# The first modulation of a two-layer diffusion step: pairs of modulation tiles go through TensorE amid the first chunk of the input projection

## The chip, the cores and the metric

The kernel runs on one core of a Trainium2 chip. Its engines work side by side, each through its own list of instructions, and wait for each other on semaphores: TensorE (PE) multiplies matrices into PSUM, VectorE (DVE) and ScalarE (ACT) work element by element, GpSimd (POOL) helps, and SyncE (SP) issues most of the transfers (DMA). The metric is the device time of one execution in microseconds, lower is better; the time of a kernel is the median of several runs.

## The reference

One step of a backbone with two layers over 512 latent and 128 context tokens (640 in all) of width 1024. What matters here is how a layer begins:

```python
def adaln(cond, w_ada, b_ada):
    m = jax.nn.silu(cond) @ w_ada + b_ada
    return jnp.split(m[:, None, :], 6, axis=-1)
def modulate(x, g, shift, scale):
    return rms_norm(x, g) * (1 + scale) + shift
...
        sh_a, sc_a, g_a, sh_f, sc_f, g_f = adaln(c, w_ada[l], b_ada[l])
        h = modulate(xs, norm_mix_g[l], sh_a, sc_a)
        q_mla, c_kv, k_rope, na_q, na_k, na_v, gq, gk, gv = mixer_inputs(
            h, w_in[l], mla_q_norm_g[l], mla_kv_norm_g[l], w_q_up[l], gqa_q_norm_g[l], gqa_k_norm_g[l])
```

There are two conditions, `c` for the latent tokens and `c_ctx` for the context tokens. `m` has 6 x 1024 features, here 48 tiles of 128: tiles 0 to 7 are the shift and tiles 8 to 15 the scale of the first norm. The input projection `h @ w_in` takes 1024 features to 1824 columns.

## The kernel before

All activations are kept with features on the partitions: `x` is eight feature tiles of 128 x 640. `h` goes into `hT` as two parts, a high one and a low one (`h` minus the high part), and so do the weights (`wi`), and every dense product is three matmuls (`split_mm`, lines 773 to 775: high x high, high x low, low x high). The projection has six chunks of 304 columns. Chunk 0 runs feature tile by feature tile over five row tiles of 128 tokens, in five banks of PSUM, so tile k can be used as soon as `h_ready` says that it is there; it has 8 x 5 x 3 = 120 matmuls. Chunks 1 to 5 run row tile by row tile, 24 matmuls each.

A modulation tile is 128 features of `m` for both conditions. There are two ways to get it. VectorE's `ada(l, t)` (L1672) multiplies the tile's weights, 128 x 1024, with the silu of one condition, which lies on every partition (`silu_c`), and adds up along the row: two dots for a tile. TensorE's way is a product with the condition as the weights of two columns (`silu_k`) and 256 features streaming past it over eight feature tiles of the input: a row of 256 results on two partitions (`ada_rows`, L914). ScalarE copies the row from PSUM (L1405), and a small product with the identity turns it into columns (`rows_to_columns`, L922). In float32 each such product is two passes, so eight products stand as 16 in the trace.

In the opening of layer 0 ten of the 16 tiles (`BY_PE = 10`) go through TensorE as five pairs and six (`FIRST`) through VectorE. ScalarE squares `x`, VectorE adds the squares up (L1825, L1828), TensorE sums over features (`token_sums`, L781), ScalarE takes the root, VectorE the reciprocal, and TensorE spreads it over all partitions (`spread_rstd`, L789). Then VectorE adds the bias to all 16 tiles at once, makes the scale (`coefs`), and `modulated` makes tn = x times the reciprocal (L1719), hf = tn * coef + shift (ScalarE L1294, or VectorE L1726 for tiles 0, 4 and 7), the high part (L1302) and the low part (L1657). Loads of the opening stand in SP's queue by hand: pairs, `x`, the six tiles' weights and the first chunk's weights in turn.

During chunks 1 to 5 VectorE computes 24 more modulation tiles (`REST`), a group for each chunk (`REST_AT`), behind the split of that chunk's weights (`wi_split`).

Of the kernel before, what the change touches and what calls it, by code (L numbers as in the profile page):

```python
# [25 lines left out]
P = 128  # L26
# [25 lines left out]
RING1, RING2 = 8, 3  # L52
BY_PE = 10
FIRST = list(range(BY_PE, ADA1))
GATE = list(range(40, NADA))
REST = list(range(ADA1, GATE[0]))
REST_AT = [0, 0, 5, 10, 15, 20, 24]
# [3 lines left out]
ORDER = [list(range(BY_PE, NADA)), NEXT + REST]  # L61
# [11 lines left out]
NORM_BANK = [5, 3, 1, 3, 1]  # L73
# [163 lines left out]
def build(nc, a, out):  # L237
    ctx = ExitStack()
    with ctx:
# [57 lines left out]
        s7 = ExitStack()  # L297
        ada_n = sb("ada_n", [P, BY_PE // 2, KD, 2 * P], F32, s7)
        s7.close()
# [32 lines left out]
        ada_w1 = sb("ada_w1", [P, RING1 - RING2, DM], F32, s2)  # L332
        sb("pad_z", [P, NT * IN_COLS - 6 * T - (RING1 - RING2) * DM], F32, s2)
# [15 lines left out]

        s4 = ExitStack()  # L350
# [15 lines left out]
        spare = ada_w1[:, len(FIRST) - RING2:, :].rearrange("p a b -> p (a b)")  # L366
        silu_k = spare[:, BY_PE * P:BY_PE * P + 2 * KD].rearrange("p (k q) -> p k q", q=2)
        rows = spare[0:2, 0:BY_PE * P]

# [11 lines left out]
        ada_n_in = [sem(f"ada_n_in{i}") for i in range(BY_PE // 2)]  # L381
        rows_ps = sem("rows_ps")
        rows_done = sem("rows_done")
        acc_first = sem("acc_first")
        ada_n_ps = sem("ada_n_ps")
        silu_done = sem("silu_done")
        ada_in = [sem(f"ada_in{i}") for i in range(RING1)]
# [133 lines left out]
        def ring_of(l, t):  # L521

            if l and t not in REST:
                return 2, NEXT.index(t)
            return (RING2, t - ADA1) if t in REST else (RING1, t - BY_PE)

        def ada_slot(l, t):

            slot = slot_of(l, t)
            if l == 0 and t >= GATE[0] and slot >= 6:  # L530
                where = ada_g[:, slot - 6]
            elif slot < 2:
                where = ada_w[:, slot]
            elif slot < RING2:
                where = ada_wq[:, slot - 2]
            else:
                where = ada_w1[:, slot - RING2]
            return where, ada_in[slot], 16 * (len(slot_users(l, t)) + 1), dot_at(l, t)

        def slot_of(l, t):  # L540

            if l == 0 and t >= GATE[0]:
                return (6, 7, 0, 1)[(t - GATE[0]) % 4]
            ring, n = ring_of(l, t)
            return n % ring

# [70 lines left out]
        def _(sp):  # L617
# [30 lines left out]
            for l in range(DEPTH):  # L648

                if l == 0:  # L650
                    def ada_n_load(i):
                        sp.dma_start(ada_n[:, i], a["w_ada_first"][i]).then_inc(ada_n_in[i], 16)

                    def x_load(i):
                        sp.dma_start(x[:, 4 * i:4 * i + 4, :], a["x"][4 * i * P:4 * (i + 1) * P, :]
                                     .rearrange("(k p) n -> p k n", p=P)).then_inc(x_in[i], 16)
                    sp.dma_start(silu_k, a["condT"]).then_inc(cond_k_in, 16)
                    ada_n_load(0)
                    sp.dma_start(silu_c[:], a["cond"].unsqueeze(0).broadcast_to([P, 2, DM])).then_inc(cond_in, 16)
                    ada_load(0, FIRST[0])  # L660
                    ada_load(0, FIRST[1])
                    x_load(0)
                    ada_n_load(1)
                    ada_load(0, FIRST[2])
                    x_load(1)
                    ada_load(0, FIRST[3])
                    ada_n_load(2)
                    ada_load(0, FIRST[4])
                    ada_n_load(3)
                    wi_load(l, 0)  # L670
                    ada_n_load(4)
                    ada_load(0, FIRST[5])
# [7 lines left out]
                if l:  # L680
# [4 lines left out]
                    sp.wait_ge(cond_in, 48)  # L685
# [9 lines left out]
                for c in range(1, IC):  # L695
# [4 lines left out]
                    for t in REST[REST_AT[c]:REST_AT[c + 1]]:  # L700
                        ada_load(l, t)
# [69 lines left out]
        def _(pe):  # L771
# [136 lines left out]
            def ada_rows(pair):  # L908

                pe.wait_ge(ada_n_in[pair], 16)  # L910
                if pair >= 2:
                    pe.wait_ge(rows_done, pair - 1)
                for k in range(KD):
                    m = pe.matmul(ps[0:2, 2 + 2 * (pair % 2), 0:256], silu_k[:, k], ada_n[:, pair, k, :],  # L914
                                  start=k == 0, stop=k == KD - 1, skip_group_check=True)
                m.then_inc(rows_ps, 1)

            def rows_to_columns(pair):

                pe.wait_ge(rows_done, pair + 1)  # L920
                for t in range(2 * pair, 2 * pair + 2):
                    m = pe.matmul(ps[:, 3, 2 * t:2 * t + 2], rows[:, t * P:(t + 1) * P], ident[0:2, 0:2],  # L922
                                  start=True, stop=True, skip_group_check=True)
                m.then_inc(ada_n_ps, 1)

            pe.wait_ge(ones_set, 1)
            for l in range(DEPTH):
                if l == 0:
                    pe.wait_ge(silu_k_done, 1)
                    for pair in range(3):  # L930
                        ada_rows(pair)
                    pe.wait_ge(acc_first, KD - 1)
                    token_sums(0, rstd, True, True).then_inc(ss_done, 1)
                    ada_rows(3)
                    pe.wait_ge(const_in, 16 * 5)
                    for pair in range(3):
                        rows_to_columns(pair)
                    spread_rstd(0)
                    ada_rows(4)
                    for pair in range(3, 5):  # L940
                        rows_to_columns(pair)

                for c in range(IC):
                    pe.wait_ge(wi_ready, l * IC + c + 1)
                    if c == 0:

                        for k in range(KD):
                            pe.wait_ge(h_ready, l * 2 * KD + k + 1)
                            for t in range(NT):
                                m = split_mm(ps[:, t, 0:ICW], hT[:, k, 0, t * P:(t + 1) * P], hT[:, k, 1, t * P:(t + 1) * P],  # L950
                                             wi[:, 0, 0, k, :], wi[:, 0, 1, k, :], k == 0, k == KD - 1)
                                if k == KD - 1:
                                    m.then_inc(z_ps, 1)
                        continue
# [303 lines left out]
        def _(sc):  # L1258
# [23 lines left out]

            def modulated(l, nrm):
                base = l * 2 * KD + nrm * KD
                own = (2 * l + nrm) * (KD - len(HF_DVE))
                sc.wait_ge(coef_done, l * 2 + nrm + 1)
                for k in range(KD):
                    sc.wait_ge(tn_ready, base + k + 1)
# [9 lines left out]
                    else:  # L1298
# [3 lines left out]
                        sc.activation(hT[:, k, 0], own_hf, ACT.Copy).then_inc(h_hi, 1)  # L1302

# [87 lines left out]
            for l in range(DEPTH):  # L1391
                if l == 0:
                    sc.wait_ge(cond_k_in, 16)
                    sc.activation(silu_k, silu_k, ACT.Silu).then_inc(silu_k_done, 1)
                    for dst, src in ((b_ada, a["b_ada"]), (norm_g, a["norm_g"]), (ident, a["ident"]), (fin_g, a["fin_g"]),
                                     (qn_g, a["qn_g"])):
                        sc.dma_start(dst[:], src).then_inc(const_in, 16)
                    sc.wait_ge(cond_in, 16)
                    sc.activation(silu_c[:], silu_c[:], ACT.Silu).then_inc(silu_done, 1)
# [3 lines left out]
                    def rows_out(pair):  # L1403
                        sc.wait_ge(rows_ps, pair + 1)
                        sc.activation(rows[:, 256 * pair:256 * pair + 256], ps[0:2, 2 + 2 * (pair % 2), 0:256], ACT.Copy).then_inc(rows_done, 1)  # L1405

                    def first_square(k):
                        if k >= 2:
                            sc.wait_ge(acc_first, max(1, k - 2))
                        sc.activation(sq[:, k % 2], x[:, k], ACT.Square).then_inc(sq_ready, 1)  # L1410
# [974 lines left out]
```

## Time and profile before

| | |
|---|---|
| median of 3 runs | 1703.88 us (1703.1 to 1705.22) |
| the profiled execution's own time | 1701.98 us |
| its span, first to last instruction | 1700.2 us |
| mean granted TensorE clock | 0.985 |
| TensorE busy | 1631.1 us (96%) |
| VectorE busy | 1310.9 us (77%) |
| ScalarE busy | 781.5 us (46%) |
| moved by DMA | 223.79 MB, mean 132 GB/s |

The busy shares are means over stages that differ. What a change of the opening is worth is read from the order of events in the opening, and from whether the stages behind it wait for TensorE, VectorE or a transfer. A time in a row is counted from the start of the span.

### The profile page before, as it was taken

What the parts mean: (1) busy time and instruction counts of PE and PEld (TensorE: products, weight loads), DVE (VectorE), ACT (ScalarE), POOL (GpSimd) and SP (SyncE); (2) the same over time, 40 slices, a digit from 0 to 9 for tenths busy, and PEclk for the clock granted to TensorE, in tenths of its full rate; (3) what the DMA queues carried; (4) which work ended last, traced back from release to release, by engine and by line L of the source; (5) the groups of instructions that cost most, each with busy time, mean ns of one, the idle gap of its engine ahead of it and who ended that gap; (6) DMA issues with size and microseconds to landing.
All of it is one profiled execution on the core that took longest, in us unless ns stands there. A gap on an engine that the chain in (4) does not pass through costs nothing.

```text
span 1700.2 us, 28338 instructions
## 1 busy us (share of the span) xinstructions
PE 1631.1 (96%) x10942; PEld 1560.1 (92%) x10942; DVE 1310.9 (77%) x2309; ACT 781.5 (46%) x1489; POOL 398.5 (23%) x438
## 2 busy tenths in 40 slices
PE   6999989999999999999999989999999999999997
PEld 2998878889999999999999977888999999999997
DVE  5897788877988888888869877887387777677764
ACT  3534767852633333333352476687363333333332
POOL 0033554310012221212114073632001221121111
PEclk8999999999999999999989999999999999999998
DMA  9562000065177777777537310001606666666651
GB/s 369 193 229 65 10 3 1 1 218 167 40 181 193 207 202 191 188 192 195 161 131 241 118 45 1 3 1 39 198 1 156 178 148 162 153 175 166 154 129 62
DMA packets 114138, 223.79 MB, mean 132 GB/s; under 512 B 7488, under 2 KB 39040, under 8 KB 113024
## 3 DMA queue, kind: packets, MB, share of 16 engines
q1 hardware_dynamic: 90800, 177.90, 30.5%
q0 software_dynamic: 22240, 44.14, 15.6%
q8 instruction: 49, 0.80, 0.2%
q10 hardware_dynamic: 1008, 0.61, 0.1%
q14 instruction: 41, 0.34, 0.1%
HBM read 218.01 MB, written 3.57 MB: 130 GB/s over the span
## 4 chain that ended last, share of the span: by engine, by line
PE 84%; DVE 8%; ACT 3%; issue 2%; DMA 1%; POOL 1%; SPq 1%; POOLq 0%; DVEq 0%; ACTq 0%
PE ps L773 24%; PE ps L775 24%; PE ps L774 24%; DVE ps L1672 3%; PE ps L1041 3%; PE ps L1011 1%; PE ps L781 1%; PE ps L1013 1%; PE ps L858 1%; PE ps L816 1%; DMA ada_n<-in_w_ada_first 1%; DVE hT L1657 1%; DVE negmax L1909 1%; PE ps L914 1%; PE ps L796 1%
## 5 line engine op out<-in xcount | busy, mean ns | idle before, releaser
L773 PE MATMUL ps<-act,dhi 128*128 128x320 f32 x704 | 217.8, 309 | 0.0
L775 PE MATMUL ps<-act,dlo 128*128 128x320 f32 x704 | 217.5, 309 | 0.0
L774 PE MATMUL ps<-act,dhi 128*128 128x320 f32 x704 | 217.5, 309 | 0.0
L2036 DVE SCALAR_TENSOR_TENSOR x<-ps,mod,x 128x512 f32<-128x512 f32 x352 | 170.4, 542 | 42.4 <-PE ps L775 42.4
L773 PE MATMUL ps<-hS,whi 128*128 128x320 f32 x640 | 197.8, 309 | 0.0
L774 PE MATMUL ps<-hS,whi 128*128 128x320 f32 x640 | 197.8, 309 | 0.0
L775 PE MATMUL ps<-hS,wlo 128*128 128x320 f32 x640 | 197.8, 309 | 0.0
L1657 DVE TENSOR_TENSOR wlo<-wraw,whi 128x1024 fp32r<-128x1024 f32 (+3 forms) x166 | 192.0, 1166 | 5.1 <-POOL wraw L2296 5.1
L773 PE MATMUL ps<-hT,whi 128*128 128x320 f32 x608 | 188.0, 309 | 2.2 <-DVE hT L1657 2.2
L775 PE MATMUL ps<-hT,wlo 128*128 128x320 f32 x608 | 187.9, 309 | 0.0
L774 PE MATMUL ps<-hT,whi 128*128 128x320 f32 x608 | 187.9, 309 | 0.0
L1562 ACT ACTIVATE whi<-wraw 128x1024 fp32r<-128x1024 f32 (+1 forms) x160 | 146.8, 946 | 50.2 <-POOL wraw L2296 18.6
L773 PE MATMUL ps<-wi,hT 128*128 128x304 f32 x480 | 146.6, 305 | 4.7 <-DVE hT L1657 4.1
L775 PE MATMUL ps<-wi,hT 128*128 128x304 f32 x480 | 146.0, 304 | 0.0
L774 PE MATMUL ps<-wi,hT 128*128 128x304 f32 x480 | 145.5, 303 | 0.0
L588 POOL TENSOR_SCALAR probs<-probs,rinv 128x640 f32<-128x640 f32 (+2 forms) x128 | 101.8, 796 | 149.5 <-DVE rinv L569 148.4
L773 PEld LDWEIGHTS ps<-act,dhi 128*128 128x128 f32 x704 | 132.1, 188 | 0.6 <-DVE x L2036 0.5
L774 PEld LDWEIGHTS ps<-act,dhi 128*128 128x128 f32 x704 | 132.2, 188 | 0.0
L775 PEld LDWEIGHTS ps<-act,dlo 128*128 128x128 f32 x704 | 132.2, 188 | 0.0
L2296 POOL TENSOR_TENSOR wraw<-wraw 128x512 f32<-128x512 f32 x40 | 63.7, 1592 | 271.3 <-PE ps L775 109.4
L1657 DVE TENSOR_TENSOR pT<-ps,pT 128x512 fp32r<-128x512 f32 (+2 forms) x176 | 109.1, 621 | 14.7 <-ACT pT L1494 13.8
L774 PEld LDWEIGHTS ps<-hS,whi 128*128 128x128 f32 x640 | 120.1, 188 | 0.0
(265 smaller groups left out, 4331.3 us busy)
## 6 DMA issues: line engine op xcount, KB each, us to landing
ada_w<-in_w_adaT SPq DMA_DIRECT2D x65, 512.0 KB, 5.1
draw<-in_w_down SPq DMA_DIRECT2D x22, 1024.0 KB, 6.0
wraw<-in_up_q SPq DMA_DIRECT2D x22, 768.0 KB, 6.6
wraw<-in_gate_q SPq DMA_DIRECT2D x20, 768.0 KB, 4.4
wraw<-in_gate_q POOLq DMA_DIRECT2D x20, 768.0 KB, 7.2
wraw<-in_up_q POOLq DMA_DIRECT2D x20, 768.0 KB, 7.1
wi_raw<-in_w_in SPq DMA_DIRECT2D x12, 1216.0 KB, 6.9
wraw<-in_gate_q SPq DMA_DIRECT2D x20, 512.0 KB, 3.4
```

The lines of the kernel that those rows point to most:

```text
L588: po.tensor_scalar(t, t, rinv[:, u:u + 1], 1.0, ALU.mult, ALU.mult).then_inc(p_ready, 1)
L773: pe.matmul(dst, lh, rh, start=start, stop=False, skip_group_check=True)
L774: pe.matmul(dst, lh, rl, start=False, stop=False, skip_group_check=True)
L775: return pe.matmul(dst, ll, rh, start=False, stop=stop, skip_group_check=True)
L781: m = pe.matmul(ps[:, bank, 2 * t:2 * t + 2], tile[:, t * P:(t + 1) * P], ones[:, 0:2], start=first and t == 0, stop=last, skip_group_chec ...
L796: pe.matmul(ps[:, bank, 0:tile.shape[-1]], tile[:, 0:P], tile, start=True, stop=True, skip_group_check=True)
L1041: m = pe.transpose(ps[:, 4 + n % 2, i * P:(i + 1) * P], probs[:, g % 2, i, pos:pos + P], ident[:])
L1562: sc.activation(whi[:, g], wraw[:, g], ACT.Copy).then_inc(quarter_hi[m], 1)
L1657: return ve.tensor_tensor(dst, src, f(hi), ALU.subtract)
L1672: i = ve.scalar_tensor_tensor(out=junk, in0=w, scalar=1.0, in1=c[:, q], op0=ALU.mult, op1=ALU.mult, accum_out=mod[:, l, t, q:q + 1])
L2036: i = ve.scalar_tensor_tensor(out=x[:, o, c0:c1], in0=y[:, 512 - HALF + c0:512 - HALF + c1], scalar=mod[:, l, 5 * KD + o, q:q + 1], in1=x[ ...
L2296: po.tensor_tensor(wraw[:, 7 * m + S4], wraw[:, 7 * m + S2], wraw[:, 7 * m + A12], ALU.add).then_inc(s4_done[m], 1)
```

## The change

- All 16 tiles of the first norm go through TensorE, as eight pairs of another make: pair k has shift tile k and scale tile 8 + k, the two that feature tile k of `h` needs. The weights are stored accordingly on the host side.
- Pairs use four buffers (`SLOTS`) in turn, two in `ada_n0` and two in `ada_n1`. The load of pair k waits until the rows of pair k - 4 are done.
- Three pairs are computed ahead of chunk 0. Within it, TensorE computes the rows of pair k + 3 after feature tile k, and turns the rows of pair k + 2 between its row tiles 1 and 2. ScalarE's row copy stands behind the high part of tile k, VectorE's bias and scale of tile k + 1 ahead of the low part of tile k (`first_mod`, `first_modulated`).
- The silu of the conditions on all partitions (`silu_c`) is no longer loaded: TensorE spreads it from `silu_k` with the identity, 16 products (`spread_silu`), and ScalarE copies it out of PSUM. Keep-warm products on the identity (24, 6 and 3) are added.
- The spread reciprocal is copied from PSUM to `rstd` and read from there. The first weights are split in two halves.
- SP's queue begins with the condition, the identity and `x`, then pair 0, the first weights, and the other seven pairs.
- `REST_AT` of layer 0 moves one tile from the first group to the last.

The core of the diff:

```diff
-REST_AT = [0, 0, 5, 10, 15, 20, 24]
+REST_AT = [[0, 0, 4, 9, 14, 19, 24], [0, 0, 5, 10, 15, 20, 24]]
...
+                    sp.dma_start(silu_k[:], a["condT"]).then_inc(cond_k_in, 16)
+                    sp.dma_start(ident[:], a["ident"]).then_inc(ident_in, 16)
+                    for i in range(2):
                         sp.dma_start(x[:, 4 * i:4 * i + 4, :], a["x"][4 * i * P:4 * (i + 1) * P, :]
                                      .rearrange("(k p) n -> p k n", p=P)).then_inc(x_in[i], 16)
...
+                    first_load(0)
                     wi_load(l, 0)
-                    ada_n_load(4)
-                    ada_load(0, FIRST[5])
+                    for k in range(1, KD):
+                        first_load(k)
...
+            def first_rows(k):
+
+                pe.wait_ge(ada_n_in[k % SLOTS], 16 * (k // SLOTS + 1))
+                if k:
+                    pe.wait_ge(rows_done, k)
+                for j in range(KD):
+                    m = pe.matmul(ps[0:2, 5, 0:2 * P], silu_k[:, j], first_w(k)[:, j, :], start=j == 0, stop=j == KD - 1,
+                                  skip_group_check=True)
                 m.then_inc(rows_ps, 1)
...
+            def first_chunk(l, k):
+
+                pe.wait_ge(h_ready, l * 2 * KD + k + 1)
+                for t in range(NT):
+                    if t == 2 and l == 0 and k + 2 < KD:
+                        first_columns(k + 2)
+                    m = split_mm(ps[:, t, 0:ICW], hT[:, k, 0, t * P:(t + 1) * P], hT[:, k, 1, t * P:(t + 1) * P],
+                                 wi[:, 0, 0, k, :], wi[:, 0, 1, k, :], k == 0, k == KD - 1)
...
-                    pe.wait_ge(silu_k_done, 1)
-                    for pair in range(3):
-                        ada_rows(pair)
+                    spread_silu()
+                    keep_warm(4, ident[:], 24)
+                    first_rows(0)
                     pe.wait_ge(acc_first, KD - 1)
                     token_sums(0, rstd, True, True).then_inc(ss_done, 1)
-                    ada_rows(3)
-                    pe.wait_ge(const_in, 16 * 5)
-                    for pair in range(3):
-                        rows_to_columns(pair)
+                    first_columns(0)
+                    keep_warm(2, ident[:], 6)
                     spread_rstd(0)
-                    ada_rows(4)
-                    for pair in range(3, 5):
-                        rows_to_columns(pair)
-
-                for c in range(IC):
+                    first_rows(1)
+                    keep_warm(2, ident[:], 3)
+                    first_columns(1)
+                    first_rows(2)
+                    pe.wait_ge(wi_half_ready, 1)
+                    pe.wait_ge(mod_done, 2)
+                    for k in range(KD):
+                        if k == KD // 2:
+                            pe.wait_ge(wi_ready, 1)
+                        first_chunk(l, k)
+                        if k + 3 < KD:
+                            first_rows(k + 3)
...
+                    if l == 0 and nrm == 0 and k + 2 < KD:
+                        rows_out(k + 2)
```

TensorE's list from its first instruction to the first matmul of chunk 0, before (-) and now (+). L914 before is a product of a row, L922 a turning; now L914 is the spreading of the silu, L796 a keep-warm product, L924 a product of a row and L938 a turning:

```order
-L914 MATMUL ps<-ada_n,ada_w 2x256 x24
+L914 MATMUL ps<-ident,silu_k 128x128 x16
+L796 MATMUL ps<-ident 128x128 x24
+L924 MATMUL ps<-ada_n,silu_k 2x256 x8
 L781 MATMUL ps<-ones,rstd 128x2 x5
-L914 MATMUL ps<-ada_n,ada_w 2x256 x8
-L922 MATMUL ps<-ident,ada_w 128x2 x6
+L938 MATMUL ps<-ident,rows 128x2 x2
+L796 MATMUL ps<-ident 128x128 x6
 L789 MATMUL ps<-ident,rstd 128x128 x5
-L914 MATMUL ps<-ada_n,ada_w 2x256 x8
-L922 MATMUL ps<-ident,ada_w 128x2 x4
```

Three of the five pairs stood ahead of the sums (L781) and two behind; now one pair stands ahead of the sums. Two more of the eight follow before the chunk, and five are inside it, where before there were only the 120 matmuls.

ScalarE's list of the change from the root of the sums to the high part of tile 2 (L1316 copies a row out of PSUM, L1453 and L1455 make the high part of half the first weights, L1457 copies the spread reciprocal, L1332 and L1340 make `h`):

```order
L1309 ACTIVATE rms<-ps,eps 128x5
L1455 ACTIVATE wi<-wi_raw 128x1216
L1457 ACTIVATE rstd<-ps 128x640
L1316 ACTIVATE rows<-ps 2x256
L1460 DMA rope<-in_rope 128x768
L1460 DMA mask<-in_mask 128x160
L1332 ACTIVATE hT<-tn,mod,coef 128x512
L1332 ACTIVATE hT<-tn,mod,coef 128x128
L1316 ACTIVATE rows<-ps 2x256
L1332 ACTIVATE hf<-tn,mod,coef 128x512
L1332 ACTIVATE hf<-tn,mod,coef 128x128
L1340 ACTIVATE hT<-hf 128x640
```

Before, all row copies came ahead of the first high part; now ScalarE waits for a row after each of the tiles 0 to 5.

VectorE's list of the change from the last bias and scale to the first dots of chunk 1 (L1772 adds the bias, L1775 makes the scale, L1810 is tn, L1816 hf, L1691 the low parts):

```order
L1772 TENSOR_TENSOR mod<-ps,b_ada 128x2x2
L1775 SCALAR_TENSOR_TENSOR coef<-mod,norm_g 128x2
L1810 TENSOR_TENSOR tn<-x,rstd 128x640
L1816 TENSOR_SCALAR hf<-tn,coef,mod 128x512
L1816 TENSOR_SCALAR hf<-tn,coef,mod 128x128
L1691 TENSOR_TENSOR hT<-hf,hT 128x640 x2
L1691 TENSOR_TENSOR wi<-wi_raw,wi 128x2432
L1706 SCALAR_TENSOR_TENSOR ps,mod<-ada_w,silu_c 128x1024 x4
```

The low parts of tiles 6 and 7 (x2) come behind the bias and scale of tile 7, so behind the turning of the last pair's rows.

## Rows read from the trace of the kernel before

**Rows 1.** The page: span, and the chain that ended last by engine.

```profile
span 1700.2 us, 28338 instructions
...
PE 84%; DVE 8%; ACT 3%; issue 2%; DMA 1%; POOL 1%; SPq 1%; POOLq 0%; DVEq 0%; ACTq 0%
```

**Rows 2.** Busy time by stretch: length, PE, PEld, DVE, ACT, POOL, clock, DMA share, GB/s.

```profile
5.00:10.00 5.00, 3.68 (x9) 1.15 (x10) 0.00 (x0) 1.12 (x1) 0.00 (x0) 1.00 1.01 405
...
0.00:47.30 47.30, 29.76 (x121) 12.67 (x121) 27.16 (x42) 16.95 (x24) 0.44 (x6) 0.88 0.99 361
47.30:53.40 6.10, 6.10 (x25) 6.10 (x26) 5.20 (x9) 5.79 (x10) 0.00 (x0) 0.52 1.05 395
...
53.40:150.20 96.80, 96.80 (x697) 96.67 (x696) 88.49 (x130) 37.44 (x72) 19.51 (x18) 1.00 0.48 159
```

**Rows 3.** Timeline of TensorE in the opening: start, duration, operation, idle before.

```profile
6.32 6.52 PE L914 MATMUL ps<-ada_n,ada_w 128*2 128x256 f32 x16 [6.32 <-DMA ada_n<-in_w_ada_first]
...
26.11 5.17 PE L914 MATMUL ps<-ada_n,ada_w 128*2 128x256 f32 x16 [2.43 <-DMA ada_n<-in_w_ada_first]
...
31.21 1.28 PE L781 MATMUL ps<-ones,rstd 128*128 128x2 f32 x10
...
35.97 1.50 PE L922 MATMUL ps<-ident,ada_w 2*128 2x2 f32 x12
37.39 1.38 PE L789 MATMUL ps<-ident,rstd 128*128 128x128 f32 x10
...
47.26 0.59 PE L773 MATMUL ps<-wi,hT 128*128 128x304 f32 x1 [3.88 <-DVE hT L1657]
```

**Rows 4.** The chain that ended last: start, share in the chain, operation.

```profile
32.49 3.54 PE ps L914 x16
...
38.77 3.54 PE ps L914 x16
```

**Rows 5.** Timeline of TensorE in layer 1, at a granted clock of 0.50.

```profile
868.63 2.33 PE L789 MATMUL ps<-ident,rstd 128*128 128x128 f32 x10
```

**Rows 6.** Timeline of VectorE and ScalarE in the opening.

```profile
2.50 0.22 ACT L1394 ACTIVATE ada_w<-ada_w 128x16 f32<-128x16 f32 x1 [0.47 <-DMA ada_w<-in_condT]
...
27.24 3.61 DVE L1828 TENSOR_TENSOR rstd<-rstd,sq 128x640 f32<-128x640 f32 x4
...
31.32 0.37 ACT L1405 ACTIVATE ada_w<-ps 2x256 f32<-2x256 f32 x1 [1.56 <-PE ps L914]
...
43.78 0.17 DVE L1686 SCALAR_TENSOR_TENSOR coef<-mod,norm_g 128x16 f32<-128x16 f32 x1
...
44.90 1.20 ACT L1294 ACTIVATE hT<-tn,mod,coef 128x512 fp32r<-128x512 f32 x2 [2.18 <-DVE tn L1719]
...
46.30 0.82 DVE L1657 TENSOR_TENSOR hT<-hf,hT 128x640 fp32r<-128x640 f32 x1
...
47.64 0.74 ACT L1302 ACTIVATE hT<-hf 128x640 fp32r<-128x640 f32 x1
...
57.76 0.80 DVE L1726 TENSOR_SCALAR hf<-tn,coef,mod 128x512 f32<-128x512 f32 x2
```

**Rows 7.** Groups by line, whole span: a copy of 512 columns from PSUM.

```profile
L1336 ACT ACTIVATE K<-ps 64x512 fp32r<-64x512 f32 x36 | 21.3, 591 | 22.3 <-PE ps L775 12.5 <-PE ps L858 9.6
```

**Rows 8.** Timeline of ScalarE and VectorE, from chunk 0 to the stage's end.

```profile
58.99 2.22 ACT L1276 ACTIVATE wi<-wi_raw 128x2432 fp32r<-128x2432 f32 x1
...
61.24 2.69 DVE L1657 TENSOR_TENSOR wi<-wi_raw,wi 128x2432 fp32r<-128x2432 f32 x1 [1.22 <-ACT wi L1276]
...
70.20 0.42 ACT L1443 ACTIVATE z<-ps 128x304 f32<-128x304 f32 x1 [0.71 <-PE ps L775]
...
149.03 0.34 DVE L1884 SCALAR_TENSOR_TENSOR z<-z,stat,kv_g 128x128 f32<-128x128 f32 x1
...
150.36 0.42 ACT L1443 ACTIVATE z<-ps 128x304 f32<-128x304 f32 x1 [2.92 <-PE ps L775]
...
151.16 0.28 DVE L1657 TENSOR_TENSOR K<-kc_na,K 64x128 fp32r<-64x128 f32 x1 [1.78 <-ACT K L1310]
```

More of the change, by code:

```diff
@@ L380, in build @@
         silu_k_done = sem("silu_k_done")
-        ada_n_in = [sem(f"ada_n_in{i}") for i in range(BY_PE // 2)]
+        ident_in = sem("ident_in")
+        silu_ps = sem("silu_ps")
+        ada_n_in = [sem(f"ada_n_in{i}") for i in range(SLOTS)]
         rows_ps = sem("rows_ps")
         rows_done = sem("rows_done")
+        mod_done = sem("mod_done")
+        coef_k = sem("coef_k")
+        rstd_copied = sem("rstd_copied")
+        wi_half_hi = sem("wi_half_hi")
+        wi_half_ready = sem("wi_half_ready")
         acc_first = sem("acc_first")
@@ L386, in build @@
         silu_done = sem("silu_done")
-        ada_in = [sem(f"ada_in{i}") for i in range(RING1)]
+        ada_in = [sem(f"ada_in{i}") for i in range(5)]
         ada_done = sem("ada_done")
@@ L524, in ring_of @@
                 return 2, NEXT.index(t)
-            return (RING2, t - ADA1) if t in REST else (RING1, t - BY_PE)
+            return RING2, t - ADA1
         def ada_slot(l, t):
             slot = slot_of(l, t)
-            if l == 0 and t >= GATE[0] and slot >= 6:
-                where = ada_g[:, slot - 6]
-            elif slot < 2:
+            if slot < 2:
                 where = ada_w[:, slot]
@@ L536, in ada_slot @@
             else:
-                where = ada_w1[:, slot - RING2]
+                where = ada_g[:, slot - RING2]
             return where, ada_in[slot], 16 * (len(slot_users(l, t)) + 1), dot_at(l, t)
@@ L906, in queries, with spread_silu @@
                 m.then_inc(qm_ps, 1)
[L908 to L915, printed above, removed]
-                m.then_inc(rows_ps, 1)
[L918 to L922, printed above, removed]
+            def spread_silu():
+                pe.wait_ge(silu_k_done, 1)
+                pe.wait_ge(ident_in, 16)
+                for q in range(2):
+                    for k in range(KD):
+                        m = pe.matmul(ps[:, 2 * q + k // 4, (k % 4) * P:(k % 4 + 1) * P], silu_k[:, k, q:q + 1].broadcast_to([P, P]),
+                                      ident[:], start=True, stop=True, skip_group_check=True)
+                    m.then_inc(silu_ps, 1)
@@ new lines, in first_rows, with first_columns @@
+            def first_rows(k):
[5 more added lines that the diff above has]
+                                  skip_group_check=True)
+                m.then_inc(rows_ps, 1)
+            def first_columns(k):
+                pe.wait_ge(rows_done, k + 1)
+                if k == 0:
+                    pe.wait_ge(silu_done, 1)
+                else:
+                    pe.wait_ge(mod_done, k)
+                if k == 2:
+                    pe.wait_ge(rstd_copied, 1)
+                for half in range(2):
+                    m = pe.matmul(ps[:, FIRST_BANK[k], 2 * half:2 * half + 2], rows[0:2, k % 2, half * P:(half + 1) * P], ident[0:2, 0:2],
@@ L1281, in rms, with rows_out @@
                 sc.activation(rms5[:], sums, ACT.Sqrt, scale=1.0 / DM, bias=eps[:]).then_inc(rms_ready, 1)
+            def rows_out(k):
+                sc.wait_ge(rows_ps, k + 1)
+                if k >= 2:
+                    sc.wait_ge(ada_n_ps, k - 1)
+                sc.activation(rows[0:2, k % 2], ps[0:2, 5, 0:2 * P], ACT.Copy).then_inc(rows_done, 1)
             def modulated(l, nrm):
```

204 lines of the change are left out of this document (114 added, 90 removed).

## The prediction

> **What bounds the kernel now.** I read the profile in five steps. The chain that ended last [rows 1] lies on TensorE for 84% of a span of 1700.2 us, so a microsecond that TensorE starts its dense work later is a microsecond at the end unless something else gives way. The busy times by stretch [rows 2] show where it is not dense: in the first 47.3 us it is busy 29.8 us, from 53.4 to 150.2 us it is busy all 96.8 us, in 697 matmuls of 0.139 us each. The timeline of TensorE [rows 3] shows what the first 47 us are: five products of the condition with a pair of modulation tiles (L914, 16 passes each), three of them behind a wait for their DMA, then the sums, the spreading of the rms, the turned rows (L922), and at 47.26 us the first chunk of the input projection. ScalarE starts to copy the first row tile of chunk 1 at 70.20 us [rows 8]; that is 24 matmuls of 0.139 us or 3.34 us after chunk 1 began, so chunk 0 ended at 66.9 us. It took 19.6 us for 120 matmuls, since its first 6.1 us ran at a granted clock of 0.52 [rows 2]. From there to 150.3 us TensorE never waits. The figure to forecast is therefore the end of chunk 0, 66.9 us now.
>
> **What the change moves.** Before, five pairs (ten tiles) go through TensorE and six tiles through VectorE. Now all 16 tiles go through TensorE, as eight pairs. Three pairs stand before the chunk and five inside it. One pair takes 3.54 us at full clock [rows 4]. VectorE's twelve dots cost TensorE nothing before; the three pairs more cost it 10.6 us. Against this TensorE's waits for DMA in the opening go, the first chunk starts earlier, and it runs at full clock.
>
> **The start of the chunk.** The first wait is for the identity tile, now second on SP's queue. The condition, issued at 0.75 us, is used at 2.50 us [rows 6]; the identity is issued some 0.4 us later. I take 4.0 us, between 3.5 and 5.5. TensorE then has 16 spreads and 24 keep-warm products, 80 passes of 128 columns. At half clock such a pass takes 0.21 us (ten in 2.33 us, with 0.42 us for the last) [rows 5], at full clock 0.114 us (1.38 us for ten) [rows 3]. How long it stays at the lower level of 1.2 GHz: after a wait the row products began slow at 6.32 us and 26.11 us and the first chunk at 47.26 us [rows 3]; the group at 26.11 took 5.17 us instead of 3.54, so some 3.3 us were slow, and the chunk was slow for 6.1 us. I take 4.8 us: 22 slow passes, then 58 in 6.6 us, done at 15.4 us. The first pair follows and ends at 18.9 us. DMA is not in the way: at 405 GB/s [rows 2] x, the first pair and the first weights (4.9 MB) are in by some 16 us, the pairs follow each 2.6 us, so the third is in by 22 us.
>
> ScalarE and VectorE run beside it. Half of the spread silu is there at 7.4 us, all by 9.8 us; four copies from PSUM of 0.59 us [rows 7] end at 11.1 us. Then come eight squares and seven sums at 0.90 us each (3.61 us for four) [rows 6]: the last sum ends at 19.0 us. So both chains meet at 19 us. From there everything is in one line on TensorE: sums 1.28, two columns 0.5 (12 passes of turning take 1.50 us), twelve keep-warm passes 1.4, spreading the rms 1.3, pair two 3.54, six passes 0.7, columns 0.5, pair three 3.54. The chunk starts at 31.8 us, 15.4 us earlier than now. The rms copy on ScalarE, the first product with x, half the weight split and the first h tile end before that: by the rows of 0.74 to 0.82 us [rows 6] h of tile 0 is ready near 30.4 us.
>
> **The length of the chunk.** 120 matmuls at 0.139 us are 16.7 us, five pairs at 3.54 us are 17.7 us, six turnings at 0.5 us are 3.0 us. For tiles 0 to 4 TensorE needs 6.1 us a tile, while ScalarE needs 1.94 us for h (1.20 and 0.74) and 0.37 us for the row copy, VectorE 1.6 to 2.4 us and two small operations of 0.2 us [rows 6]; they are covered. The cover ends at tile 6. The last pair ends at 62.5 us, its row copy is followed on ScalarE by h of tile 6, and on VectorE by columns at 63.9, coefficients 0.4, tn 0.8, hf 0.8 and the low half 0.8 us: 66.7 us, where TensorE has been free since 65.1 us. That is a wait of 1.6 us. Sum 39.0 us, end of chunk 0 at 70.8 us. Weights of chunk 1 are split on ScalarE only after the last h, 2.22 us, and on VectorE, 2.69 us [rows 8]: 66.4 + 2.2 + 2.7 = 71.3 us, so TensorE waits another 0.5 us. It begins chunk 1 at 71.3 us instead of 66.9: **4.4 us later**. Moved loads: SP's queue waits for the fourth pair before the last pair's load (about 41 us), and behind it stand the weights of chunk 1, nine small tables, wq and the next tiles' loads. The weights are wanted at 66 us and the tiles at 71 us, so this costs nothing unless they come 20 us late.
>
> **After it.** VectorE begins its split at 68.6 us instead of 61.2 us, 7.4 us later, while TensorE is 4.4 us later. VectorE's 24 tiles of this stage are the same, one of them moved from the first group to the last. It ended the normalisation at 149.4 us and did its first key piece at 151.2 us [rows 8], so it had 1.8 us; it is now 3.0 us later relative to TensorE and 1.2 us late for a small piece, with more idle time right behind. I take nothing for it, with 1.2 us as the upper bound. The rest of the program waits for the end of the stage as before.
>
> Sum +4.4 us, and 0.5 us for some ten handovers between engines that I have taken as free. The profiled execution took 1701.98 us, 1.78 us over its span, and lies 1.9 us under the median of the runs, 1703.88 us. Its own time with the change would be 1706.9 us, the median 1708.8 us.
>
> **A place where rule and trace differ.** The recorded clock says 1.00 for 5 to 10 us [rows 2], yet the 16 passes that began at 6.32 us took 6.52 us [rows 3], 0.41 us each, where 16 at 2.4 GHz take 3.54 us, so the record is no help in the opening and the level was 1.2 GHz. The Trainium skill (TensorE: Matmul & The Clock Gate, What's actually happening) says that the default state is throttled and activity releases it; by that rule the opening starts slow, and the trace's pace agrees. By the rule the sum is +4.4 us, by the recorded clock the opening would be 2.2 us shorter and the sum +2.2 us.
>
> **The rivals.**
> *The clock falls once more* (chance 0.20). Near 19 us TensorE has sums and columns of two elements' width, 1.8 us, and a short wait. Before, a wait of 2.43 us at 26.11 us was enough to make the next 3.3 us slow [rows 3]; but the sums at 31.21 us, with pairs on both sides, kept full clock. If it falls, 3.4 to 5 us run at half pace: +1.7 to 2.5 us, time 1711.
> *VectorE ends the stage* (0.14). The 1.2 us above bite, or a load for its dots is late: 1710.
> *A shorter opening* (0.20). The slow stretch is short, or the wait before tile 6 vanishes because VectorE is quicker there: 1.5 to 2.5 us less, 1706 to 1707, which is no difference that can be told.
> *Faster* (0.06). The row products cost less inside the dense stream than alone, because their weights have two columns. The five would have to take 2.66 us each to break even and under 2.0 us to be faster by over 0.2%; then the time is under 1700.5. For it speaks only that none stood between dense matmuls; against it, that the two at full clock took 3.54 us each in different company [rows 4].
> *The chunk starves* because pairs arrive late: part of the slower side. The third pair has 6 us in hand at 28 us.
>
> **How the numbers follow.** The forecast itself has 0.40, with 1707 to 1710 as its own range. About 0.2% (3.4 us) is what a measurement can tell from no change. Faster 0.06; within 0.2% the shorter opening and the lowest edge of the forecast, 0.23; slower 0.71. The range goes from 1704.5 (all lower bounds: identity at 3.5, short slow stretch, no wait at tile 6) to 1713 (clock falls, identity at 5.5 us).
>
> **What would show it.** First chunk starting near 32 us; row products inside it at 3.5 us each; the chunk some 39 us long; chunk 1 starting at 71 us; a wait of one to two microseconds on the low half of h before tile 6; 4 to 5 us more in the span, all of it before 72 us. It is wrong if row products overlap with the dense matmuls, if the chunk starts before 27 us, or if the later stages give the time back.

## The result, and the profile after

The changed kernel takes 1712.64 us (median; one run of 4135 us was disturbed and is left out), the kernel before, on the same chip, 1703.1 us. The ratio is 1.0062, 95% interval 1.0049 to 1.0075, so 8.3 to 12.8 us more. The prediction said 1708.8 us. The sign was right and the time lies in the range, but the loss was forecast at 4.9 us: the medians differ by 9.5 us, about twice that.

The page of the changed kernel: span, busy time, and the chain that ended last by engine.

```profile
span 1710.2 us, 28667 instructions
...
PE 1652.5 (97%) x11100; PEld 1577.1 (92%) x11100; DVE 1294.5 (76%) x2299; ACT 784.8 (46%) x1497; POOL 395.5 (23%) x438
...
PE 84%; DVE 9%; ACT 4%; issue 2%; POOL 1%; DMA 0%; POOLq 0%; DVEq 0%; SPq 0%; ACTq 0%
```

The span grew by 10.0 us against [rows 1], and the chain still lies on TensorE. Its busy time by stretch (columns as in [rows 2]), cut at the start of chunk 0, its end, and the end of the stage:

```profile
0.00:33.40 33.40, 29.33 (x175) 22.02 (x175) 12.12 (x19) 15.84 (x24) 0.44 (x6) 0.95 0.86 318
33.40:75.00 41.60, 40.27 (x225) 26.39 (x224) 16.02 (x31) 17.45 (x30) 0.00 (x0) 1.00 0.58 192
75.00:159.00 84.00, 83.77 (x600) 83.52 (x600) 78.34 (x116) 28.73 (x61) 19.36 (x18) 1.00 0.54 178
```

Chunk 0 begins at 33.4 us instead of 47.3 and ends at 75.0 us instead of 66.7: 13.9 us are won ahead of it and some 22 lost inside it. From there to the end of the stage the distance stays the same. These are the rows of ScalarE and VectorE that answer to [rows 8]:

```profile
72.43 2.69 DVE L1691 TENSOR_TENSOR wi<-wi_raw,wi 128x2432 fp32r<-128x2432 f32 x1 [0.88 <-ACT wi L1304]
...
73.35 2.07 ACT L1477 ACTIVATE z<-ps 128x304 f32<-128x304 f32 x5 [1.02 <-PE ps L775]
...
78.83 0.42 ACT L1477 ACTIVATE z<-ps 128x304 f32<-128x304 f32 x1 [1.27 <-PE ps L775]
...
158.99 0.42 ACT L1477 ACTIVATE z<-ps 128x304 f32<-128x304 f32 x1 [2.92 <-PE ps L775]
...
160.32 0.33 DVE L1962 SCALAR_TENSOR_TENSOR z<-z,stat,kv_g 128x128 f32<-128x128 f32 x1
160.58 0.28 DVE L1691 TENSOR_TENSOR K<-kc_na,K 64x128 fp32r<-64x128 f32 x1
```

The first copy of z of chunk 1 starts at 78.83 us instead of 70.20, the last of the stage at 158.99 instead of 150.36: 8.63 us both times. So 8.6 of the 10.0 us by which the span grew arise before the first copy of chunk 1, and this copy is the marker by which the experiments below are read.

The chain that ended last shows the line on TensorE up to chunk 0 (start, share in the chain, operation):

```profile
17.97 0.84 DVE rstd L1798
18.80 0.04 issue
18.85 1.28 PE ps L781 x10
20.13 0.53 PE ps L938 x4
20.66 2.21 PE ps L796 x12
22.87 2.07 PE ps L789 x10
24.94 3.54 PE ps L924 x16
28.48 0.87 PE ps L796 x6
29.35 0.53 PE ps L938 x4
29.88 3.54 PE ps L924 x16
33.43 0.34 PE ps L773
```

The twelve keep-warm passes and the spreading of the rms took 4.28 us where 2.7 were forecast. The busy times there say why; the granted clock is the third number from the end, 0.58:

```profile
21.00:23.00 2.00, 2.00 (x13) 2.00 (x12) 0.22 (x2) 0.53 (x1) 0.00 (x0) 0.58 1.03 426
```

Inside the chunk, TensorE's timeline over one tile and the start of the next (start, duration, operation):

```profile
34.16 0.30 PE L775 MATMUL ps<-wi,hT 128*128 128x304 f32 x1
34.38 0.60 PE L938 MATMUL ps<-ident,rows 2*128 2x2 f32 x4
34.91 0.41 PE L773 MATMUL ps<-wi,hT 128*128 128x304 f32 x1
35.16 0.30 PE L774 MATMUL ps<-wi,hT 128*128 128x304 f32 x1
...
36.12 0.30 PE L775 MATMUL ps<-wi,hT 128*128 128x304 f32 x1
36.35 3.62 PE L924 MATMUL ps<-ada_n,silu_k 128*2 128x256 f32 x16
39.90 0.41 PE L773 MATMUL ps<-wi,hT 128*128 128x304 f32 x1
40.14 0.30 PE L774 MATMUL ps<-wi,hT 128*128 128x304 f32 x1
...
40.93 0.60 PE L938 MATMUL ps<-ident,rows 2*128 2x2 f32 x4
```

Read the starts, since the durations overlap. Dense matmuls start 0.14 us apart. From the last of them to the turning it is 0.22 us, and behind the turning the first takes 0.25 us until the next; the same at the row product, 0.23 and 0.24. Each change from the dense products to the narrow ones or back (a border, below) thus costs about 0.1 us, four of them 0.4 us a tile. The period of a tile is 6.55 us (34.38 to 40.93), where the forecast had 6.1.

TensorE's waits up to 170 us (in all, times, longest):

```profile
PE ps L914 <- DMA ident<-in_ident: 3.4, 1, 3.4
PE ps L773 <- DVE hT L1691: 1.3, 1, 1.3
PE ps L858 <- DVE K L1691: 0.8, 1, 0.8
PE ps L781 <- DVE rstd L1798: 0.7, 1, 0.7
...
PE ps L773 <- DVE wi L1691: 0.2, 1, 0.2
```

The 1.3 us on the low part of h are the wait before tile 6 (at 70.53 us), forecast at 1.6. No transfer is waited for inside the chunk.

### The profile page after: what moved, and what is told of

It is laid out like the page before. It is cut to its first block, busy times and chain, and to the rows that moved or that the text cites. A ratio compares the mean times of both kernels' runs of the same rounds, so it can differ in the third digit from the quotient of the medians.

```text
span 1710.2 us, 28667 instructions
## 1 busy us (share of the span) xinstructions
PE 1652.5 (97%) x11100; PEld 1577.1 (92%) x11100; DVE 1294.5 (76%) x2299; ACT 784.8 (46%) x1497; POOL 395.5 (23%) x438
## 4 chain that ended last, share of the span: by engine, by line
PE 84%; DVE 9%; ACT 4%; issue 2%; POOL 1%; DMA 0%; POOLq 0%; DVEq 0%; SPq 0%; ACTq 0%
PE ps L773 24%; PE ps L775 24%; PE ps L774 24%; DVE ps L1706 3%; PE ps L1069 3%; PE ps L924 1%; PE ps L781 1%; PE ps L1039 1%; PE ps L1041 1%; PE ps L858 1%; PE ps L816 1%; DVE negmax L1987 1%; DVE hT L1691 1%; PE ps L796 1%; ACT probs L1428 1%
## 5 line engine op out<-in xcount | busy, mean ns | idle before, releaser
L1691 DVE TENSOR_TENSOR wlo<-wraw,whi 128x1024 fp32r<-128x1024 f32 (+3 forms) x166 | 189.7, 1153 | 7.4 <-POOL wraw L2374 7.4
L1596 ACT ACTIVATE whi<-wraw 128x1024 fp32r<-128x1024 f32 (+1 forms) x160 | 148.2, 947 | 74.4 <-DMA wraw<-in_gate_q 33.4
L1691 DVE TENSOR_TENSOR pT<-ps,pT 128x512 fp32r<-128x512 f32 (+2 forms) x176 | 109.1, 621 | 14.9 <-ACT pT L1528 13.6
```

Of the source, the lines that this page charges most:

```text
L1596: sc.activation(whi[:, g], wraw[:, g], ACT.Copy).then_inc(quarter_hi[m], 1)
L1691: return ve.tensor_tensor(dst, src, f(hi), ALU.subtract)
```

## The experiments

The theory was that TensorE's own list is the cost: five pairs of 3.55 us stand in the chunk, and the rest of the miss is the clock near 20 us and the changes between products. The rivals were that the order or a wait of another engine makes the loss, and that it lies behind the first stage. "Copy" below is the start of the first copy of z of chunk 1; all ratios are to the kernel before on the same chip, with their 95% intervals. The copy comes from one execution of each version, so a difference of some tenths of a microsecond in the opening can be that execution's own.

**Four more keep-warm products.** They fill TensorE's wait for the last sum.

```
 first_rows(0)
+keep_warm(4, ident[:], 4)
 pe.wait_ge(acc_first, KD - 1)
```

> Edit: four more keep-warm products on the identity ahead of TensorE's wait for the sum of squares (18.1 to 18.85 us in the trace of the change). The trace of the change shows the keep-warm products and the spreading of the rms from 20.6 to 24.9 us at half pace, 2.28 us each instead of 1.4 and 1.3 us. Theory A (TensorE's own list is the path, and its clock fell after the wait and the narrow products): the clock stays up, the chunk starts 1.5 to 1.8 us earlier, time 1710.5 to 1711 beside 1712.6 of the change. Rival (the clock fell because of the narrow products, 1.9 us of sums and turnings, which the edit leaves): it falls all the same and the time is 1712.6 or 0.2 more.

Ratio 1.0045 (1.003 to 1.006), copy at 78.83 us, as in the change. TensorE's timeline near 21 us shows the fall gone, and the chunk begins at 32.32 instead of 33.36 us:

```profile
21.18 1.60 PE L796 MATMUL ps<-ident 128*128 128x128 f32 x12
22.62 1.28 PE L789 MATMUL ps<-ident,rstd 128*128 128x128 f32 x10
...
69.51 0.62 PE L773 MATMUL ps<-wi,hT 128*128 128x304 f32 x1 [1.30 <-DVE hT L1692]
69.93 0.46 PE L774 MATMUL ps<-wi,hT 128*128 128x304 f32 x1
70.18 0.46 PE L775 MATMUL ps<-wi,hT 128*128 128x304 f32 x1
```

But behind the wait before tile 6 the matmuls now start 0.25 us apart, at a granted clock of 0.50 in the busy times:

```profile
70.00:72.00 2.00, 2.00 (x10) 2.00 (x10) 1.12 (x2) 1.30 (x1) 0.00 (x0) 0.50 0.01 4
```

The microsecond was won and lost again in this execution. The same wait of 1.30 us left the clock alone in the changed kernel. The chunk began 1.0 us earlier and not 1.5 to 1.8, since the identity came at 3.91 us instead of 3.35 and the sums began 0.7 us later. The clock stayed up near 21 us in all five versions with these four products. Of the seven executions without them it fell in five; it stayed up in the repeated change and in the version with pair 7 by dots, so one execution alone does not show what the products do.

**Half of each row product.** The pairs inside the chunk multiply four of eight feature tiles; half of their modulation is thus left out. Nothing else changes.

```
-for j in range(KD):
+n = KD // 2 if k >= 3 else KD
+for j in range(n):
```

> Edit: the row products of pairs 3 to 7, those within the chunk, take four of the eight feature tiles of the condition instead of eight, so the modulation of tiles 3 to 7 is left half computed. Theory A (TensorE's list is the path): each of the five is 1.77 us shorter, the chunk 8.9 us shorter, time near 1703.8. Theory B (the ring row product, row copy on ScalarE, turning, bias and scale on VectorE, h sets the pace of a tile, and TensorE follows): the rest of the ring stays, and no more than 2 us are saved, time 1710.5 or more.

Ratio 1.0004 (0.9995 to 1.0013): the loss is gone. TensorE's timeline shows the short row products:

```profile
36.24 1.89 PE L925 MATMUL ps<-ada_n,silu_k 128*2 128x256 f32 x8
...
39.10 0.60 PE L939 MATMUL ps<-ident,rows 2*128 2x2 f32 x4
...
41.09 1.89 PE L925 MATMUL ps<-ada_n,silu_k 128*2 128x256 f32 x8
```

A tile takes 4.85 us (36.24 to 41.09) and the copy is at 70.10 us, 8.73 earlier; five times half of 3.54 us are 8.9. The waits and the half-pace stretch near 20 us are still there, and so is every handover, so those alone do not make the loss. TensorE's time in the row products passes one to one into the marker, as the first theory said; the second allowed 2 us.

**The turning directly ahead of the row product.** Two changes of product a tile instead of four.

```
-if t == 2 and l == 0 and k + 2 < KD:
+if t == 2 and l == 0 and k + 2 == KD - 1:
     first_columns(k + 2)
...
 if k + 3 < KD:
+    first_columns(k + 2)
     first_rows(k + 3)
```

> Edit: the turning of the rows of pairs 2 to 6 stands at the end of the tile, straight ahead of the next row product, instead of between row tiles 1 and 2. In the trace of the change TensorE loses about 0.1 us each time it goes from dense to narrow float32 products or back, four times a tile, 0.4 us a tile in sum. Theory A: two of the four go, five times: 1.0 us less, time 1711.6. Theory B (ring of waits): turned 1.3 us later, bias, scale, tn and h come later in each tile, 1 us or more is lost a tile, time 1717 or more.

Ratio 1.0053 (1.0038 to 1.0068), which alone can't be told from the change. The trace can: copy at 77.22 us, 1.6 earlier.

```profile
35.06 0.60 PE L938 MATMUL ps<-ident,rows 2*128 2x2 f32 x4
35.59 3.62 PE L924 MATMUL ps<-ada_n,silu_k 128*2 128x256 f32 x16
...
41.41 0.60 PE L938 MATMUL ps<-ident,rows 2*128 2x2 f32 x4
```

The period is 6.35 us (35.06 to 41.41) instead of 6.55: two changes fewer, 0.2 us less, so 0.1 us for one. Over the five tiles this is 1.0 of the 1.6 us; the other 0.6 is the start of the chunk, 32.79 instead of 33.36 us, since the opening ran a little sooner in this execution. The loss of 1 us or more a tile that a ring of waits would have brought did not come.

**One, two and three pairs by VectorE.** In these, `NPE` pairs go through TensorE and the others (two tiles each) are dots on VectorE, part of them in its idle time of the opening, part inside the chunk's tiles. The edit also puts the loads of these tiles' weights between those of the pairs, and TensorE waits for the dots of the opening before chunk 0. First pair 7 alone:

```
+NPE = 7
+BY_DVE = [7, 15]
+DOTS_AT = {-1: [(7, 0)], -2: [(7, 1), (15, 0), (15, 1)]}
...
-if k + 3 < KD:
+if k + 3 < NPE:
     first_rows(k + 3)
```

> Edit: pair 7 (tiles 7 and 15) is computed by VectorE as four dots of 1.33 us, one ahead of the bias of pair 0 and three behind the reciprocal, where the trace of the change shows VectorE idle for 2.0 and 4.5 us; its row product, row copy and turning go. Theory A: TensorE loses 3.54 for the product, 0.53 for the turning, 0.4 for the changes, and most of the 1.3 us wait before tile 6, since VectorE no longer stands behind that turning: 5.0 to 5.8 us less, time 1707 to 1707.6. Theory B: the dots delay tn of tile 0 by 1 us and with it the ring, time 1712 to 1714.

Ratio 1.0032 (1.002 to 1.0044), copy at 73.23 us, 5.6 earlier, within the 5.0 to 5.8 that the first theory said. One pair fewer is 3.54 + 0.53 + 0.4 us, the waits on h shrank from 1.3 to 0.7, and the chunk began 0.85 us earlier: 1.6 us won, since the clock did not fall near 20 us in this execution, and 0.8 lost, since the sums began later (19.64 us). Together 5.9 us, 0.3 too many.

Then the change once more, beside versions with two and three pairs taken off:

> The changed kernel once more, on the chip of the next three runs, as their reference. Every theory expects 1.0062 of the time before, 8.3 to 12.8 us more. Its trace also tells whether the fall of TensorE's clock near 19 us comes in each execution, at the same place, or now and then.

Ratio 1.0063 (1.005 to 1.0075), copy at 78.23 us. The ratio repeats. In this execution the clock did not fall near 20 us, though the same wait for the last sum stands there:

```profile
19.87 1.28 PE L781 MATMUL ps<-ones,rstd 128*128 128x2 f32 x10 [0.72 <-DVE rstd L1798]
...
21.61 1.60 PE L796 MATMUL ps<-ident 128*128 128x128 f32 x12
23.05 1.28 PE L789 MATMUL ps<-ident,rstd 128*128 128x128 f32 x10
```

Its sums began 1.0 us later instead (19.87 against 18.85 us): the identity came 0.3 us later, and the first 32 passes, which spread the silu, took 6.61 us instead of 5.87. So the fall comes now and then. Without it this execution still lies 8.0 us behind the kernel before at the marker. Then the version with two pairs taken off, 6 and 7:

```
+NPE = 6
+BY_DVE = [7, 15, 6, 14]
+DOTS_AT = {-1: [(7, 0)], -2: [(7, 1), (15, 0), (15, 1)],
+           2: [(6, 0), (6, 1)], 3: [(14, 0), (14, 1)]}
```

> Edit: pairs 6 and 7 are computed by VectorE as eight dots, four in its idle time of the opening, four behind the bias and scale of tiles 3 and 4 in the chunk, where it waits 4.7 us a tile; TensorE does six pairs. Theory A (TensorE's list is the path, 4.5 us a pair): tiles 0 to 2 take 6.55 us, tile 3 2.6, the rest 2.1 us each, with about 1 us of waits on VectorE: chunk 1 begins near 66 us, as before the change (66.9), ratio to before 0.999 to 1.001. Rival (the dots put VectorE behind, ring of waits): ratio 1.002 or more.

Ratio 0.9996 (0.9987 to 1.0005), copy at 69.75 us, 0.45 ahead of the kernel before: what the first theory said. With three pairs taken off (5, 6 and 7, dots in tiles 2 to 5):

> Edit: pairs 5, 6 and 7 by VectorE as twelve dots, eight of them in the chunk; TensorE does five pairs, as many as before the change. Theory A: TensorE's list would end the chunk at 59 us, but VectorE's (23 us from 36 us on) ends h of tile 7 near 61 us and the split of the next weights near 65 us: chunk 1 begins at 64 to 66 us, ratio to before 0.998 to 1.000. Rival: each dot moved to VectorE costs what it saves on TensorE, ratio above 1.001.

Ratio 1.0016 (1.0005 to 1.0027), copy at 73.11 us: the expectation was missed. TensorE's waits up to 170 us in that kernel:

```profile
PE ps L784 <- DVE hT L1703: 5.3, 4, 3.8
```

TensorE had a pair less on its list than with two (4.5 us) and waited 5.3 us for h: VectorE had become the bound. Its timeline shows it (and TensorE's behind the longest wait):

```profile
48.53 0.16 DVE L1791 TENSOR_TENSOR mod<-ps,b_ada 128x4 f32<-128x4 f32 x1 [2.25 <-PE ps L949]
...
66.71 2.69 DVE L1703 TENSOR_TENSOR wi<-wi_raw,wi 128x2432 fp32r<-128x2432 f32 x1 [1.23 <-ACT wi L1316]
...
53.74 0.62 PE L784 MATMUL ps<-wi,hT 128*128 128x304 f32 x1 [3.79 <-DVE hT L1703]
54.16 0.46 PE L785 MATMUL ps<-wi,hT 128*128 128x304 f32 x1
54.41 0.46 PE L786 MATMUL ps<-wi,hT 128*128 128x304 f32 x1
```

Until 48.53 us VectorE waits for turned rows, since its dots in the chunk stand behind the bias of a tile; from there to 65.5 us it waits for nothing. Behind the wait of 3.79 us TensorE runs at half pace (starts 0.25 us apart), so part of what it lost to VectorE shows as slow matmuls and not as waiting. The same version with the later turning and four keep-warm products:

> Edit: e6 with the turning of pairs 2 and 3 at the end of their tiles and four keep-warm products ahead of the wait for the sum of squares. Theory A: the chunk starts 0.3 us later or earlier, no fall of the clock near 19 us, 0.4 us saved on the turnings; ratio 0.0005 to 0.001 below that of e6. If the clock is no cause, the ratio is that of e6.

Ratio 1.0015 (1.0007 to 1.0024), copy at 72.57 us, waits on h 7.2 us in five. This expectation was missed too: the ratio is that of the version before. TensorE began the chunk 1.05 us earlier (32.69 us instead of 33.74) and waited longer.

**The last combinations.** Two pairs by dots, later turning, four keep-warm products:

> Pairs 6 and 7 by VectorE's dots, the turning directly ahead of the next row product (0.19 us less for each of some four tiles, from the run that moved the turning alone) and four more keep-warm products near 19 us (1 us where the clock would fall). TensorE-list theory: first copy of z of chunk 1 near 69.0 us where two pairs by dots alone had 69.75, ratio to before 0.9985 to 0.9995, and it is the best of the versions. Rival (VectorE is the bound as soon as it has dots in the chunk, as with three pairs): the earlier TensorE only waits longer for h, the waits on h grow from 1.1 to about 2 us, and the ratio stays at 0.9996 or above.

Ratio 1.0 (0.9991 to 1.0009), copy at 71.00 us, later than without the two edits. The waits up to 170 us:

```profile
PE ps L784 <- DVE hT L1705: 3.4, 4, 1.7
```

The rival held: the waits on h grew from 1.1 to 3.4 us. The four products can account for at most the 0.5 us by which the chunk began earlier (32.38 us instead of 32.90). For the rest the likely cause, not shown by a run of its own, is the later turning: VectorE gets its columns nine dense matmuls later (1.3 us), and bias, dots, tn and h of the next tile all stand behind them. Here TensorE also waited 0.5 us for the second pair's weights, a transfer now behind those of the dots. The next run but one leaves the turning in place. All eight pairs on TensorE with both edits:

> All eight pairs on TensorE as in the change, with the later turning and the four keep-warm products, nothing moved to VectorE. TensorE-list theory: the two savings add, 1.0 us from the clock near 19 us and 1.0 to 1.6 us from fewer changes between products; chunk 1's first copy of z near 76.5 us instead of 78.83, ratio 1.0045 to 1.0055, so that some 8 us of row products remain as the price of the change. Rival (the time lies in the order and the clock, not in the products' own length): the ratio falls to 1.003 or below.

Ratio 1.0045 (1.003 to 1.0061), copy at 76.21 us, 2.6 earlier than the change, as the first theory said: 1.6 from the start of the chunk (31.79 us) and 1.0 from the borders. It has the shortest list on TensorE of the versions with eight whole pairs, and 6.0 us of the loss remain. Last, two pairs by dots with the turning left in place, the dots spread over the tiles 1 to 3, four keep-warm products:

```
-           2: [(6, 0), (6, 1)], 3: [(14, 0), (14, 1)]}
+           1: [(6, 0)], 2: [(6, 1), (14, 0)], 3: [(14, 1)]}
```

> Pairs 6 and 7 by VectorE's dots as before, with the turning where the change has it (its move left VectorE no time), the four dots inside the chunk spread one, two and one over the tiles 1, 2 and 3 instead of two and two over 2 and 3, and four more keep-warm products near 19 us. If VectorE's dots were what made TensorE wait for h, the waits on h fall from 1.1 to under 0.7 us, the first copy of z of chunk 1 is near 68.5 us (69.75 less 1.0 for the clock and 0.3 for the waits), ratio to before 0.9985 to 0.9995. Rival (the end of the chunk is held by h of tiles 5 and 6, whose coefficients come from VectorE in any case): the waits stay at 1 us or more, the copy is at 69.0 or later and the ratio 0.9995 to 1.0005.

Ratio 0.9993 (0.9982 to 1.0003), copy at 68.93 us and waits on h of 0.8 us, between what the two theories said. Against the version before it with two pairs both the turning and the dots stand elsewhere, so it is open how much each gave. It is the best version, 1.3 us ahead of the kernel before at the marker, which the timing can't tell from no change. Six pairs on TensorE are about where chunk 0 ends as early as before.

## Why the prediction was right in sign and wrong in size

The mechanism was the forecast one: an earlier start of the chunk against five row products inside it. The step that failed is the length of the chunk: the sum took the borders between dense and narrow products at nothing, beside 0.5 us for all handovers, and they measured 2.2 us. The second miss is the pace ahead of the chunk, 1.6 us, which the prediction had as a rival and not in its sum.

**The start of the chunk: 31.8 us forecast, 33.4 measured.** The identity came at 3.35 us, not 4.0, and the last sum ended at 18.8 us as forecast (19.0). The miss is one term: keep-warm and spreading took 4.28 us at half pace where the forecast had 2.7. This is the rival "the clock falls once more", with the chance 0.20 and 1.7 to 2.5 us; it cost 1.6. Behind "a short wait" of 0.72 us and 1.8 us of products of two columns, the granted clock was 0.58. In the run with four keep-warm products and in the repeated change the same 22 passes took 2.65 us (21.18 to 23.83, 21.61 to 24.26), as forecast. That the forecast start had no fall was thus a choice between two cases that both occur: of seven executions with this wait five had the fall, so the chance of 0.20 was too low. The Trainium skill (TensorE: Matmul & The Clock Gate, What's actually happening) calls the number of slow matmuls at a kernel's start run-variable for one and the same kernel. The two executions of the change agree: their first 32 passes took 5.87 and 6.61 us. That a fall near 21 us comes in one of them and not in the other is what these runs show beside it.

**The length of the chunk: 39.0 us forecast, 41.6 measured.** This is the step that failed. Dense matmuls (16.7 us) and row products (five at 3.54) were right. Taken as nothing was the change from one kind of product to the other. It measures 0.4 us a tile; with the turning at tile 5, which has no row product behind it, that is 5 × 0.4 + 0.2 = 2.2 us. The turnings took 0.53 us each instead of 0.5, which adds 0.2. The wait before tile 6 was 1.3 us instead of 1.6. Some 0.5 us remain, and they lie outside the periods of the tiles: the first matmul of the chunk and the first behind the wait take 0.24 and 0.25 us until the next, 0.1 us more than the others, and the two waits are each some 0.15 us shorter in the list than the gap in the timeline. The run with the later turning confirms the 0.1 us a change by removing two a tile.

**Chunk 1: 71.3 us forecast, 75.2 measured.** The wait for its weights was 0.2 us instead of 0.5. So +3.9 us are +1.6 from the clock, +2.6 from the chunk and −0.3 from this wait. The figure before was read 0.2 us too late: a copy starts 0.34 us after the start of its last matmul, and TensorE's timeline of the kernel before has chunk 1's first matmul at 66.66 us, not 66.9. It now begins 8.5 us later, where 4.4 were forecast. The 0.5 us for handovers was the only allowance for all of it.

**After it: nothing, as forecast.** VectorE's last piece of the normalisation starts at 160.32 us instead of 149.03, 11.3 later where TensorE is 8.6 later: 2.7 us, forecast as 3.0. Its idle time of 1.78 us ahead of the first key piece [rows 8] is used up, and the piece comes 0.8 us later relative to TensorE (1.2 was the bound). That fell into slack: TensorE's wait for K there is 0.8 us before and after. Loads moved past SP's queue were never waited for. The marker moved by 8.6 us and the timed difference is 8.3 to 12.8 us. In the profiled pair the rest of the 10.0 us, 1.4 behind the marker, appears only in layer 1 (from TensorE's first spreading of the rms there, 868.63 us before and 876.94 now, to the end of the span: 831.6 and 833.3 us), a length that lies between 831.6 and 834.0 us over all profiled executions; whether some of it belongs to the change stays open.

**The rivals.** "Faster" needed row products under 2.66 us in the dense stream; they took 3.54, as outside it. The Trainium skill (VectorE: DVE Perf Modes, The TRN2 errata) gives a matmul's length by its free size alone. The trace agrees that the number of output partitions doesn't count: a pass of 256 columns onto two partitions took 0.22 us, one of 128 columns onto 128 partitions 0.114. It does not agree in size: by the formula in that section of the Trainium skill 256 columns are 262 cycles, which I estimate at 0.11 us at 2.4 GHz, and a recorded float32 pass took twice that. "VectorE ends the stage" was wrong: what it lost there fell into slack. VectorE did become the bound in another place, inside chunk 0, once it got twelve dots. "A shorter opening" did not come, and the chunk never starved: no pair was waited for. The half row products are the direct proof of the sign: 8.9 us of TensorE's list taken away gave 8.7 us at the marker.

## What to carry to other kernels

When work is moved onto the engine that bounds the kernel, first write down the sum that it adds to that engine's list (three pairs, 10.6 us plus their turnings), and then what idle time it can fill: here TensorE was busy 29.8 us ahead of the chunk before and 29.3 now, so the 13.9 us won there are idle time. They and the 2.7 us of slow pace in the old chunk stand against 17.7 us of row products, 3.2 of turnings, 2.2 of changes, 1.3 of waiting and 0.5 beside them. Price each border between dense and narrow products by the starts in a timeline, not by the durations, and group the narrow ones. Balance by moving only as much as the other engine's idle time holds: with two pairs back on VectorE the loss was gone, with three VectorE held TensorE up by 5.3 us and the clock fell behind the longest of these waits.

## What the runs showed of the hardware that was not expected

- A change between dense matmuls (304 columns) and narrow products, in either direction, costs about 0.1 us beside the products' own time (0.22 to 0.25 us from start to start instead of 0.14). The first dense matmul behind a plain wait costs the same (70.53 to 70.78 us), so the half of the cost that falls on the way back to dense products may be that of any new start.
- Whether the clock falls after a short wait is not a property of the kernel alone. The wait of 0.6 to 0.7 us for the last sum, with 1.8 us of two-column products behind it, was followed by half pace in five of seven executions. The two without a fall are those whose first 32 passes took longest: 6.58 and 6.61 us, against 5.18 to 6.21 in the five.
- The wait of 1.3 us before tile 6 was followed by full pace in five executions (both of the change among them) and by half pace, a granted clock of 0.50, in the run that differs only by four keep-warm products. The wait of 3.8 us in the two versions with three pairs by dots was followed by half pace both times.
- In the opening the recorded clock is no help: the busy times from 3 to 9 us record 1.00, while the 32 passes that began at 3.35 us took 5.87 us, where 32 at 0.114 us are 3.7.
